# A hybrid encoder layer on one core: the start's loads and products in another order, and four unread products

## What is computed

```
mod = silu(c) @ w_ada + b_ada            # shift, scale, gate, one vector a group
h   = rmsnorm(x) * (1 + sc1) + sh1
proj = h @ w_in                          # q, k, v | hyena | two gates
attn = windowed attention with a sink logit
spec = rfft(filters(L)),  h = sin(f1 * (z @ w1 + b1)); h = sin(f2 * (h @ w2 + b2)); h @ w3, decayed
hy   = order-2 long convolution with spec
x    = x + g1 * ((sigmoid(ga) * (attn @ w_ao) + sigmoid(gh) * (hy @ w_ho)) @ w_out)
x    = x + g2 * (relu(h2 @ w_up)**2 @ w_down)
y    = rmsnorm(x) * (1 + scf) + shf
```

## Time and profile before

| | before |
|---|---|
| median of 3 runs | 1112.43 us (1112.22 to 1113.51) |
| the profiled execution's own time | 1114.14 us |
| its span | 1112.6 us |
| TensorE busy | 1092.2 us (98%) |
| VectorE busy | 802.3 us (72%) |
| ScalarE busy | 454.5 us (41%) |
| chain that ended last, TensorE's share | 93% |

### The profile page before, as it was taken

How to read it: one execution, slowest core, us unless ns; L and a number is a source line. 1 busy time by engine, 2 the same in 40 slices (tenths; PEclk the granted TensorE clock), 3 DMA queues, 4 the chain that set the end, 5 groups by cost and what they waited for, 6 DMA issues and landing times.

```text
span 1112.6 us, 16634 instructions
## 1 busy us (share of the span) xinstructions
PE 1092.2 (98%) x6304; PEld 1022.2 (92%) x6304; DVE 802.3 (72%) x1334; ACT 454.5 (41%) x792; POOL 108.9 (10%) x132
## 2 busy tenths in 40 slices
PE   6999999999999999999999999999999999999997
PEld 4787798888899999999899999999999999999886
DVE  5777699889388685556455777787978778788534
ACT  5631156665722322423246232253442526157414
POOL 2101200000334322000000000000000000000000
PEclk9999999999999999999999999999999999999998
DMA  9923454333332333753312331143333232222303
GB/s 345 394 86 117 154 189 143 129 127 114 119 123 105 119 104 124 282 153 108 110 57 95 125 121 57 57 152 99 111 103 106 95 109 91 87 76 76 95 19 115
DMA packets 45525, 138.85 MB, mean 125 GB/s; under 512 B 5051, under 2 KB 10635, under 8 KB 44556
## 3 DMA queue, kind: packets, MB, share of 16 engines
q1 hardware_dynamic: 29024, 80.21, 21.6%
q0 software_dynamic: 11376, 44.84, 11.3%
q10 hardware_dynamic: 5052, 12.81, 3.3%
HBM read 121.61 MB, written 15.74 MB: 123 GB/s over the span
## 4 chain that ended last, share of the span: by engine, by line
PE 93%; DVE 4%; DMA 1%; ACT 1%; issue 0%; ACTq 0%; DVEq 0%
PE acc_ps L750 39%; PE wk L1181 16%; PE acc_ps L1200 12%; PE acc_ps L832 12%; PE wk L1056 2%; PE acc_ps L839 1%; PE wk L991 1%; PE wk L980 1%; PE wk L970 1%; PE wk L1022 1%; PE wk L872 1%; PE wk L885 1%; DVE dot_out L1832 1%; DMA filt_zh<-in_t_z 1%; PE wk L803 1%; PE wk L890 1%
## 5 line engine op out<-in xcount | busy, mean ns | idle before, releaser
L750 PE MATMUL acc_ps<-act_hilo,w_hi 128*128 128x384 f32 x1504 | 332.5, 342 | 0.1
L750 PEld LDWEIGHTS acc_ps<-act_hilo,w_hi 128*128 128x128 f32 x1504 | 264.8, 189 | 18.8 <-issue 17.7
L750 PE MATMUL acc_ps<-act_hilo,w_lo 128*128 128x384 f32 x752 | 191.5, 335 | 0.0
L750 PEld LDWEIGHTS acc_ps<-act_hilo,w_lo 128*128 128x128 f32 x752 | 136.4, 188 | 0.0
L1200 PE MATMUL acc_ps<-hidden_hilo,act_hilo 128*128 128x384 f32 x768 | 134.6, 335 | 0.2
L1200 PEld LDWEIGHTS acc_ps<-hidden_hilo,act_hilo 128*128 128x128 f32 x768 | 133.2, 188 | 1.1 <-issue 1.1
L1741 DVE TENSOR_TENSOR w_lo<-w_raw,w_hi 128x1024 fp32r<-128x1024 f32 x61 | 76.3, 1252 | 55.1 <-ACT w_hi L1282 54.1
L1282 ACT ACTIVATE w_hi<-w_raw 128x1024 fp32r<-128x1024 f32 x61 | 64.2, 1053 | 44.3 <-PE acc_ps L750 40.9
L2198 DVE SCALAR_TENSOR_TENSOR xT<-acc_ps,modT,xT 128x512 f32<-128x512 f32 (+1 forms) x32 | 19.7, 617 | 59.7 <-PE acc_ps L832 59.5
L1832 DVE CUSTOM_DVE_ANT_0 dot_out<-dot_ring,c_rows,vecT 128x1024 f32<-128x1024 f32 x48 | 61.6, 1284 | 1.6 <-issue 0.6
L2323 DVE SCALAR_TENSOR_TENSOR xT<-acc_ps,modT,xT 128x384 f32<-128x384 f32 (+2 forms) x96 | 40.5, 478 | 28.8 <-PE acc_ps L1200 28.8
(11 more groups left out here) (301 smaller groups left out, 2026.4 us busy)
## 6 DMA issues: line engine op xcount, KB each, us to landing
w_raw<-in_w_pre SPq DMA_DIRECT2D x50, 512.0 KB, 3.5
dot_ring<-in_w_ada_cols POOLq DMA_DIRECT2D x48, 512.0 KB, 3.8
w_raw<-in_w_up SPq DMA_DIRECT2D x32, 512.0 KB, 3.7
w_raw<-in_w_down SPq DMA_DIRECT2D x16, 512.0 KB, 3.4
w_raw<-in_w_down_half SPq DMA_DIRECT2D x32, 256.0 KB, 2.7
spec<-filt_out POOLq DMA_DIRECT2D x12, 512.0 KB, 2.9
gate_spill<-gates_out ACTq DMA_DIRECT2D x16, 384.0 KB, 2.3
hy_spec<-spec SPq DMA_DIRECT2D x12, 512.0 KB, 5.6
```

The lines of the kernel that those rows point to most:

```text
L750: mm = pe.matmul(acc_ps[:, slot, 512 * h:512 * h + HALF], w[:, k, :], src[:, x, k, HALF * h:HALF * h + HALF], start=(first and i == 0), st ...
```

## The change

Loads on SP's and GpSimd's queues are issued in another order: mod piece 3 moves from GpSimd's queue to SP's and pieces 1 and 3 stand before weight tile 0, pieces 5 and 7 before weight tile 1. On ScalarE's queue the filter's inputs and weights go ahead of the identity. TensorE's, ScalarE's and VectorE's lists get another order, with the filter's argument reduction between the norm's sums; of the ten unread products six stay among the sums, and four others are put between the rows of the second mod group, into a region of PSUM that the first projection product overwrites later. The sine's table is loaded before the root's and once more later.

```diff
--- before.py
+++ after.py
@@ -476,10 +476,13 @@
             sp.dma_start(vT[:], a["vec"]).then_inc(ld_vec, 16)
             for k in range(0, KD, 2):
                 x_load(sp, k)
-            mod_load(sp, 1)
+            for p in (1, 3):
+                mod_load(sp, p)
             weights(0)
+            for p in (5, 7):
+                mod_load(sp, p)
             weights(1)
-            for p in range(5, 4 * MODS, 2):
+            for p in range(9, 4 * MODS, 2):
                 mod_load(sp, p)
             weights(2)
             weights(3)
@@ -614,7 +617,7 @@
             pool.memset(epsc[:], EPS).then_inc(ones_set, 1)
             for k in range(1, KD, 2):
                 x_load(pool, k)
-            for p in (0, 2, 3, *range(4, 4 * MODS, 2)):
+            for p in range(0, 4 * MODS, 2):
                 mod_load(pool, p)
             for p in range(sum(MRING), 4 * MODS):
                 pool.wait_ge(ld_mod[p], 16)
@@ -904,34 +907,39 @@
                 if k == KD - 1:
                     mm.then_inc(acc_ready, 1)
 
+            pe.wait_ge(ld_filt, 32)
+            filt_mlp(0)
             pe.wait_ge(ld_ident, 16)
             turn_c()
-            pe.wait_ge(ld_filt, 32)
-            filt_mlp(0)
             pe.wait_ge(ones_set, 2)
-            for k in range(2, KD - 1):
+            for k in range(2, 6):
                 pe.wait_ge(n_acc, k)
-                warm(2)
+                if k == 3:
+                    pe.wait_ge(f_sin, 1)
+                    filt_mlp(1)
+                else:
+                    warm(2)
+            for k in range(2):
+                mod_row(0, k)
             norm_sum(0)
-            for k in range(KD):
+            for k in range(2, KD):
                 mod_row(0, k)
             norm_spread(0)
             mod_turn(0)
             for k in range(4):
                 mod_row(1, k)
-            pe.wait_ge(f_sin, 1)
-            filt_mlp(1)
+            warm(4, acc_ps[:, 0, 0:256])
             for k in range(4, KD):
                 mod_row(1, k)
             first(0, 0)
             mod_turn(1)
             first(0, 1)
+            first(1, 0)
             for k in range(KD):
                 mod_row(2, k)
-            first(1, 0)
+            first(1, 1)
             mod_turn(2)
             first(0, 2)
-            first(1, 1)
             for k in range(KD):
                 mod_row(3, k)
             first(0, 3)
@@ -1267,9 +1275,9 @@
 
         @block.scalar
         def _(act_e):
+            act_e.dma_start(zh[0:33, :], a["t_z"]).then_inc(ld_filt, 16)
+            act_e.dma_start(fw12[:], a["filt_w12"]).then_inc(ld_filt, 16)
             act_e.dma_start(ident[:], a["t_ident"]).then_inc(ld_ident, 16)
-            act_e.dma_start(fw12[:], a["filt_w12"]).then_inc(ld_filt, 16)
-            act_e.dma_start(zh[0:33, :], a["t_z"]).then_inc(ld_filt, 16)
             act_e.dma_start(sink[:], a["attn_sink"].partition_broadcast(P)).then_inc(ld_rope, 16)
 
             def split_w(t, s=None, count=None, to=None, used=None):
@@ -1348,7 +1356,7 @@
             act_e.wait_ge(ld_vec, 16)
             act_e.activation(csig[:], vT[:, V_C:V_C + 16], ACT.Sigmoid).then_inc(csig_done, 1)
             act_e.wait_ge(ones_set, 2)
-            act_e.activation(rs[:, 0:1], epsc[:], ACT.Sqrt).then_inc(sqrt_set, 1)
+            act_e.activation(es[:, 0, 0:1], epsc[:], ACT.Sin)
             act_e.wait_ge(c_turned, 1)
             act_e.activation(crow[0:16], wk[0:16, 1536:1536 + P], ACT.Copy).then_inc(c_row, 1)
             act_e.wait_ge(c_row, 1)
@@ -1360,21 +1368,23 @@
                     act_e.wait_ge(m_turned, 1)
                 act_e.activation(mrow[:, 512 * (g % 3):512 * (g % 3) + 512], mod_bank(g), ACT.Copy).then_inc(m_rows, 1)
 
-            for k in range(KD):
+            for k in range(4):
                 square(k)
+            act_e.wait_ge(f_arg, 1)
+            act_e.activation(h1[:], fb[0:64, :], ACT.Sin).then_inc(f_sin, 1)
+            for k in range(4, KD):
+                square(k)
+            act_e.activation(rs[:, 0:1], epsc[:], ACT.Sqrt).then_inc(sqrt_set, 1)
             act_e.wait_ge(sqrt_set, 1)
             norm_std(0)
-            act_e.activation(es[:, 0, 0:1], epsc[:], ACT.Sin)
+            mod_rows(0)
             split_w(0)
-            mod_rows(0)
-            split_w(1)
-            act_e.wait_ge(f_arg, 1)
-            act_e.activation(h1[:], fb[0:64, :], ACT.Sin).then_inc(f_sin, 1)
             norm_h(0)
             norm_hi(0)
             norm_h(1)
             norm_hi(1)
             mod_rows(1)
+            split_w(1)
             norm_h(2)
             norm_hi(2)
             norm_h(3)
@@ -1879,13 +1890,17 @@
                 chain(dve.scalar_tensor_tensor(fb[h], fk[h], -TWO_PI_C, fb[h], ALU.mult, ALU.add))
                 dve.tensor_scalar(fb[h], fb[h], 3.1415925, -3.1415925, ALU.min, ALU.max).then_inc(f_arg, 1)
 
-            for k in range(KD):
-                norm_acc(k)
             arg_first(0)
             arg_turns(0)
+            norm_acc(0)
+            arg_rest(0)
+            norm_acc(1)
+            arg_clamp(0)
+            for k in range(2, KD):
+                norm_acc(k)
+            arg_first(1)
             norm_rstd(0)
-            arg_rest(0)
-            arg_clamp(0)
+            arg_turns(1)
             norm_t(0)
             dve.wait_ge(ba1_done, 1)
             dve.wait_ge(c_saved, 16)
@@ -1896,7 +1911,6 @@
             norm_t(2)
             norm_lo(1)
             mod_out(1)
-            arg_first(1)
             split_w(1)
             norm_t(3)
             norm_lo(2)
@@ -1904,7 +1918,6 @@
             norm_lo(3)
             mod_out(2)
             norm_t(5)
-            arg_turns(1)
             norm_lo(4)
             norm_t(6)
             norm_lo(5)
```

## The result

The changed kernel takes 1120.64 us (median of six executions, 1120.45 to 1120.85); the kernel before took 1112.54 (median of six, 1111.25 to 1113.51). The ratio is 1.0074 (95% interval 1.0061 to 1.0086): 8.1 us slower, where 1117.0 (4.6 slower) was forecast and 1120.5 was the range's end. The direction was right, the size was not.

A forecast was written before the change was run, and what follows sets the result against it. The front before 56.53 us was taken to bound the kernel, with TensorE full behind it. 7.3 - 1.3 - 1.4 = 4.6 us later gave 1118.7 profiled, less 1.7 to the median: 1117.0 us, range 1110.8 to 1120.5.

The forecast's parts named there:

- The base: Step from the profiled execution to the median: 1.7 us taken off, giving 1117.0 us.
- The sum up to the profiled execution: Front's end 4.6 us later, at 61.1; profiled execution 1118.7 us instead of 1114.14.
- piece one: Start of the kernel to the norm's root: root at 28.3 us instead of 20.98, 7.3 us later.
- piece two: Norm's root to first projection product: 7.3 us instead of 8.64, 1.3 us back.
- piece three: First projection product to the third weight tile's products: 25.5 us instead of 26.91, 1.4 us back.
- half of the 3.5 us at clock 0.51: Low-clock stretch behind the 37.38 us turn: half of it counted, less new stalls, toward the 1.4 us gain.
- each microsecond moves it by about half: Before the norm's root: each microsecond the clock rises earlier or later shifts the root by about half.
- The early bound of that rise: Earliest time for TensorE's clock rise, 22.9 us; the late bound was 27.6 and 26 was taken.
- the quick case: Rival: filter weights land at 3.3 us, identity at 4.6, so 1110.7 us, faster than before; chance 0.16.
- the other path: VectorE's slice and scale, ScalarE's norm_h and copy, low part: ends at 35.5 us, so the unread products cost nothing.
- The loads' order: Front's large loads: second weight tile lands at 31.1, wanted at 37; piece 11 about 35, wanted at 42; not deciding.
- The clock staying low: Rival: sparse fillers and thin work keep TensorE's clock low until 33 us, another 3.5 us, 1120.5; chance 0.10.

The follow-up runs named there:

- The second trace: The kernel before, unchanged, profiled once more: 1112.08 us (11 executions), ratio 1.0001; the profiled execution took 1111.76 us.
- the fillers in the gap: The changed kernel with six more unread products on TensorE right behind the turning of c: 1118.95 us, ratio 1.0066.
- the queue: The kernel before with only ScalarE's queue reordered (filter inputs first, identity third) and the filter's first product ahead of the turning of c: 1115.2 us.
- the rest: The change minus filter work between sums and minus ScalarE's queue order, against the kernel before: 1116.5 us with new SP and GpSimd loads, 1115.36 with old.

## Why the prediction was right in its mechanism and wrong in its size

**The base, the step that failed.** "The median shown is 1112.43, 1.7 below the profiled one, so 1117.0 us is the forecast." The measured 1120.64 lies 3.6 above that. The sum up to the profiled execution missed by 2.1 (1118.7 for 1120.8): piece one 0.5, piece two 0.7, piece three nothing, the rest of the span 0.7, and 0.2 more outside the span. The step to the median missed by another 1.5, the largest single term: it took off 1.7, and the median is 0.2 below the profiled execution. The 1.7 us by which the profiled execution of the kernel before lies above its median are no overhead that any kernel has. The second trace, 2.4 us shorter, differs in a late input (9.7 for 8.1), a later rise of the clock and the fall at 38.2, and the change touches all three: it sets its own input times, and its clock stays up behind 38 us. Its six executions lie within 0.4 us of each other. I subtracted the 1.7 from a kernel that doesn't have it. The same fault is in piece three: "half of the 3.5 us at clock 0.51" was counted as a gain, but by their mean clock most executions of the kernel before (seven of these eleven, 50 of 82) have no such fall to give back. Against the second trace of the kernel before the pieces are +9.1, -1.2, +0.4 and +0.6 behind them, 8.9 us of span; against the one in front +7.8, -0.6, -1.4 and +0.7, 6.5 us. The medians' 8.1 lies between.

**Piece one** (7.3 later by the forecast, 7.8 measured against the same trace). The chain of steps holds. Inputs at 7.9 (8.5 forecast), identity at 10.8 (11.5), VectorE's list of 13.4 us as counted, last sum at 24.14 (24.9). The clock rose at 26.97 (26), and "each microsecond moves it by about half" gives the 0.5 of the root. The early bound of that rise, 22.9, rests on no row, and no run of the changed order without added fillers or earlier inputs came near it (26.25 to 28.3). Two small slips changed nothing: 25.8, 0.9 and 1.33 make 28.0 and not 28.2, and the range's lower end should be the quick case's 1110.7. That the clock is a term of its own is shown by the fillers in the gap (3.1 us earlier with the same VectorE list), that VectorE's order is the other by the filter work alone (1121.54).

**Piece two** (7.3 forecast, 8.02). The mechanism holds: the unread four stand beside the other path and cost nothing in time. What was mis-sized is the price of the mod rows. Six of them behind the root took 1.91 us, where I took 0.24 each from the earlier trace rows (x16 in 1.92), 1.44 in all. Each row uses a quarter of the array's columns, and the traces show four running side by side: after the change the first four start at 28.63 and take 1.06 us together, the last two start at 29.51 and take 1.03; in the kernel before two lots of four take 1.07 and 1.04. So six rows cost what eight cost, and the two moved ahead of the sums save nothing here, which fits the run with those rows moved alone (1112.55). That is 0.4 us ahead of the point where the two paths part, and the remaining 0.3 is small gaps between the steps. The unread four took 1.99 instead of 1.7, which doesn't count, as without them the first product is 8.03 behind the root.

**Piece three** (25.5 forecast, 25.48). That it came out to 0.1 us is luck. The stalls were 0.18, 0.49 and 0.46 us where 0.6, 0.5 and 0.8 were counted, 0.8 less, and the work took 24.35 us of TensorE (the stage from 36.80) where 23.65 was summed, 0.7 more. The 1.4 us back are the fall of the clock in the one trace in front: the second trace has 25.12 here, less than the changed kernel. The loads' order decides nothing, as forecast. The rest of the span took 0.7 us more than before (1056.83 for 1056.11); in the profiled executions of all kernels it lies between 1055.9 and 1057.4, and its cause stays open.

**The rivals.** Quick inputs: no. The identity (64 KB) took 8.6 us as the third entry and `sink` (4 KB) 11.2 us, where the identity alone in front took 2.4. By the Trainium skill, "DMA: Bandwidth & Descriptors", section "Anatomy of one DMA — SWDGE (gpsimd) path", a transfer takes about 2.0 us plus its bytes over 436 GB/s. The page fits this for GpSimd's path, which the prediction left out, and these inputs are on ScalarE's queue; here the identity as the first entry is near it and the later entries are not. Even with the inputs ahead of x the change loses 5.8 us. The clock staying low: half true, it rose 1 us later than forecast, not 7.

**What the parts do to each other.** Each in the kernel before, the filter work between the sums costs 9.2 us over its base, the queue 2.9, the rest 3.0 with the old loads and 4.5 with the new; together 8.1, not 15 or more. Three meetings of the parts are seen in the traces, and how much each gives back wasn't measured. The queue's new order brings the filter product to 7.6 to 8.2 us in every trace that has it, where the old order has 8.1 to 9.8; the filter work needs that and the rest doesn't. The filter work alone has the fall of the clock in three executions of four, by their mean clock; in the whole change it is gone, and taking out the unread four brings it back in two of four. And the filter's second argument, moved forward, frees the low part. Why only some executions of one kernel have the fall of the clock isn't settled: late inputs go with it in the two traces of the kernel before, but the run of the rows ahead alone has its product at 9.53 us and no fall.

## What to carry to other kernels

Before a difference is summed on a median, ask of each microsecond between the profiled execution and the median what it is; what the change removes or replaces must not be subtracted twice, and a second profile of the same kernel shows which stalls are of the kernel and which of that execution. Slack of an engine early in the span isn't free room: work put there that hangs on a late input carries the lateness to all that stands behind it. A kernel's parts, timed one by one, can cost twice what they cost together.

## What was not expected of the hardware

- Two times of the same binary go with the mean clock: of 82 executions of the kernel before, 49 of the 50 at 0.997 or 0.998 took 1110.98 to 1112.54 us, the 32 at 0.996 or 0.995 1112.45 to 1114.39.
- The clock fell to 0.5 without a long pause of TensorE ahead of it (1.29 us was the longest): in the run with the early fillers it fell at 26.7 after a stretch of 10.30 us in which TensorE was busy for 8.23, the last of it one-column sums and 32-column rows. Around the wait of 1.6 us for the second weight tile's low part it fell in two traces (at 34.3 and 34.7) and not in two others. With four products of 256 columns that nobody reads in the right place, the trace shows no fall, and six executions of six lie within 0.4 us of each other.
- Products on 32 columns run four at a time when they use different quarters of the array: two take 1.03 us, four take 1.06.
- A small load's landing isn't set by its bytes: 64 KB took 2.4 us as the first entry, 7.4 us as the third of SP's queue ahead of that queue's x slices, 8.6 us as the third of ScalarE's.
